# Expert input rows of a hybrid decoder step, picked by an indirect load instead of a selection product

## The reference, cut to what matters

```python
def _hier_moe(h, lp):                      # h: (tokens, 1024); 4 groups of 8 experts
    ...
    g_sel = jnp.argmax(g_logits, axis=-1)
    ...
    top_p, top_i = lax.top_k(jax.nn.softmax(e_logits, axis=-1), MOE_TOPK)      # 2 experts per token
    comb = p_group * top_p / jnp.sum(top_p, axis=-1, keepdims=True)
    expert = g_sel[:, None] * MOE_PER_GROUP + top_i
    w_tok = jnp.sum(jax.nn.one_hot(expert, MOE_EXPERTS) * comb[..., None], axis=1)
    gate = jnp.einsum('td,edf->tef', t, lp['w_exp_gate'])     # (32, 1024, 256)
    up = jnp.einsum('td,edf->tef', t, lp['w_exp_up'])         # (32, 1024, 256)
    act = jax.nn.silu(gate) * up * w_tok[..., None]
    out = jnp.einsum('tef,efd->td', act, lp['w_exp_down'])    # (32, 256, 1024)
```

## Time and profile before

| | |
|---|---|
| median of 3 runs | 901.95 us (899.47 to 902.05) |
| profiled execution | 901.02 us, of which the profile's span is 899.3 us |
| TensorE busy | 780.3 us (87%) |
| mean granted clock of TensorE | 0.935 of full |
| moved by DMA | 189.43 MB, of which 96 loads of 1024 KB are expert weights |

### The profile page before, as it was taken

How to read it: one execution, slowest core, us unless ns; L and a number is a source line. 1 busy time by engine, 2 the same in 40 slices (tenths; PEclk the granted TensorE clock), 3 DMA queues, 4 the chain that set the end, 5 groups by cost and what they waited for, 6 DMA issues and landing times.

```text
span 899.3 us, 21936 instructions
## 1 busy us (share of the span) xinstructions
PE 780.3 (87%) x9281; PEld 558.2 (62%) x9282; DVE 263.5 (29%) x731; ACT 222.0 (25%) x522; POOL 79.3 (9%) x187
## 2 busy tenths in 40 slices
PE   2679999999876689998988997569999999999984
PEld 2577777876664466776766775325556555655643
DVE  0044404411253465645611212431111111111123
ACT  1331131127413421521550003401111111111116
POOL 7000000010113210000000000011111111111100
PEclk9969999999977789999999999758999999999997
DMA  7826779994437754151026087407999975898201
GB/s 247 222 85 213 270 268 331 319 320 147 113 91 187 187 141 141 48 164 48 24 77 240 0 348 300 193 1 264 415 418 408 414 325 209 333 407 329 122 3 52
DMA packets 106471, 189.43 MB, mean 211 GB/s; under 512 B 9276, under 2 KB 70409, under 8 KB 98232
## 3 DMA queue, kind: packets, MB, share of 16 engines
q1 hardware_dynamic: 106424, 188.76, 59.0%
HBM read 180.16 MB, written 8.59 MB: 210 GB/s over the span
## 4 chain that ended last, share of the span: by engine, by line
PE 81%; DVE 7%; ACT 5%; DMA 3%; issue 3%; SPq 1%; POOL 0%; ACTq 0%; DVEq 0%; POOLq 0%
PE ps L1074 16%; PE ps L495 8%; PE ps L1232 7%; PE ps L443 6%; PE ps L461 5%; PE ps L510 4%; PE ps L408 3%; PE ps L1016 3%; PE ps L387 3%; PE ps L464 2%; PE ps L391 2%; PE ps L451 2%; DMA arena<-in_w_ada 1%; ACT arena L1460 1%; PE ps L503 1%
## 5 line engine op out<-in xcount | busy, mean ns | idle before, releaser
L1074 PE MATMUL ps<-arena 128*128 128x288 f32 x576 | 144.9, 412 | 0.0
L1074 PEld LDWEIGHTS ps<-arena 128*128 128x128 f32 x576 | 109.7, 193 | 31.0 <-DMA arena<-in_w_in 0.8
L495 PE MATMUL ps<-arena 128*32 128x128 f32 x2432 | 75.8, 278 | 12.5 <-issue 11.2
L495 PEld LDWEIGHTS ps<-arena 128*32 128x32 f32 x2432 | 66.2, 112 | 28.8 <-issue 27.7
L1232 PE MATMUL ps<-arena 128*128 128x288 f32 x256 | 71.1, 422 | 4.1 <-ACT arena L1583 4.1
L443 PE MATMUL ps<-arena 128*32 128x256 f32 (+1 forms) x936 | 64.4, 388 | 8.1 <-POOL arena L367 8.1
L1232 PEld LDWEIGHTS ps<-arena 128*128 128x128 f32 x256 | 47.1, 194 | 20.4 <-issue 8.8
L721 DVE TENSOR_SCALAR level<-arena 128x288 f32<-128x288 f32 x38 | 16.3, 429 | 114.4 <-PE ps L464 114.4
L443 PEld LDWEIGHTS ps<-arena 128*32 128x32 f32 (+1 forms) x936 | 26.3, 109 | 31.3 <-issue 25.1
L461 PE MATMUL ps<-level,arena 32*128 32x256 f32 x624 | 44.7, 401 | 0.5 <-DVE arena L724 0.5
L365 POOL TENSOR_TENSOR arena<-arena 128x192 f32<-128x192 f32 x39 | 20.5, 526 | 268.0 <-PE ps L443 234.2
(11 more groups left out here) (420 smaller groups left out, 1048.5 us busy)
## 6 DMA issues: line engine op xcount, KB each, us to landing
arena<-in_w_exp_gate SPq DMA_DIRECT2D x32, 1024.0 KB, 7.9
arena<-in_w_exp_up SPq DMA_DIRECT2D x32, 1024.0 KB, 10.0
arena<-in_w_exp_down SPq DMA_DIRECT2D x32, 1024.0 KB, 9.0
arena<-in_w_ada SPq DMA_DIRECT2D x12, 2048.0 KB, 10.2
arena<-in_w_in SPq DMA_DIRECT2D x18, 1024.0 KB, 6.0
arena<-in_w_ada_final SPq DMA_DIRECT2D x4, 2048.0 KB, 14.9
arena<-in_w_in SPq DMA_DIRECT2D x16, 512.0 KB, 4.0
arena<-in_state_ssm_rec SPq DMA_DIRECT2D x8, 512.0 KB, 6.8
```

Source lines behind the costliest of these rows:

```text
L495: l = mm(ps[CW * q:CW * (q + 1), 5, 0:P].rearrange("p (g f) -> p g f", g=2), xwin[:, at:at + CW], gate_up[:, :, k, f:f + HF], start=(k == ...
L1074: l = mm(ps[:, 2 + 2 * sl + m, 0:TOK], w_ring[sl][:, k, m * P:(m + 1) * P], HN[:, k, :], start=(k == 0), stop=(k == KT - 1))
```

## The change

The token rows `h2_tok` are stored to a memory tensor `h2_rows` of 1152 rows of 256 values (four rows for each token). VectorE makes row numbers `idx` from the place table. GpSimd fetches the 128 rows of a window by an indirect load into one of two buffers `xgs`, two windows ahead, and ScalarE copies them to `xg2`. The mask products and `picked_rows` are gone. `combined` stands behind the gate and up product. Windows are counted in pairs. The accumulators are cleared right behind the sums of the second norm, with `xT` as the other operand. The logits are transposed after the first 8 of the 24 token transposes, which now go through two banks. A seventh buffer `ex[6]` takes the place of `h2_tok` and of the routing's scratch, which moves elsewhere; its gate and up loads are issued once the rows are stored, its down load once the place tables are made. `sq3` takes the final squares.

```diff
-ESLOT = 6
+ESLOT = 7
...
         xg, q = carve(3 * DH * D, 2 * P)
+        xgs = (xg, carve(3 * DH * D + 8 * P + 2 * TOK, 2 * P)[0])
...
+        xg2, q = carve(q, 2 * P)
...
+        for at in (0, EXW, MIX, MIX + EXW, ex_at, ex_at + EXW, ex_at + 2 * EXW):
             wgu, at = carve(at, 2 * KT, FF)
-            wd, at = carve(at, FT, D)
+            wd, _ = carve(at if len(ex) < 6 else h2_at, FT, D)
...
+        assert at <= MIX
...
+        h2_rows = nc.dram_tensor("h2_rows", [4 * TOK, 2 * P], F32, kind="Internal").ap()
...
+            e.wait_ge(S("h2_tok"), 6)
+            for t, (o, p) in enumerate(TILES):
+                store(h2_rows[4 * o:4 * (o + p), :].rearrange("(p q) n -> p (q n)", q=4), h2_tok[0:p, t, :])
+            rec_stores.append(stores[0])
+            e.wait_ge(S("stored"), 16 * rec_stores[1])
+            wgu, wd = ex[6]
+            load(wgu[:, 0:KT, :], wg_[:, 6], "ex_ld6")
+            load(wgu[:, KT:2 * KT, :], wu_[:, 6], "ex_ld6")
+            e.wait_ge(S("count_mm"), 3)
             e.wait_ge(S("tab"), 1)
+            load(wd, wd_[:, 6], "ex_ld6")
             with e.Fori(1, E // ESLOT) as i:
...
+            for q in range(4):
+                link(g.memset(quarter[CW * q:CW * (q + 1)], float(q)))
...
-            def picked(n):
-
-                g.tensor_tensor(out=pm6, in0=B6, in1=A6[:, :, bass.ds(n, 1)].broadcast_to([P, 6, CW]), op=ALU.mult).then_inc(S("pm6"), 1)
-                e.wait_ge(S("pm6"), n + 1)
-                g.tensor_tensor(out=pm, in0=pm6[:, 0:3, :], in1=pm6[:, 3:6, :], op=ALU.add).then_inc(S("pm"), 1)
-
-            e.wait_ge(S("placed"), 1)
-            picked(0)
-            chunks = e.value_load(tab[0:1, 1, E - 1:E], min_val=1, max_val=MAXWIN)
-            with e.Fori(0, chunks) as c:
-                e.wait_ge(S("pick_mm"), c + 1)
-                e.wait_ge(S("pm"), c + 1)
-                picked(c + 1)
+            def gathered(rows, u):
+
+                g.indirect_dma_start(xgs[u], None, h2_rows, bass.IndirectOffsetOnAxis(rows, 0)).then_inc(S(f"xg_ld{u}"), 16)
+
+            e.wait_ge(S("stored"), 16 * rec_stores[1])
+            e.wait_ge(S("idx"), 1)
+            for u in range(2):
+                gathered(idx[:, u:u + 1], u)
+            e.wait_ge(S("tab"), 1)
+            pairs = e.value_load(tab[0:1, 2, 0:1], min_val=1, max_val=MAXWIN // 2)
+            with e.Fori(0, pairs) as c:
+                for u in range(2):
+                    e.wait_ge(S("xg"), c * 2 + (u + 1))
+                    g.tensor_copy(out=idx_now[:, u:u + 1], in_=idx[:, bass.ds(c * 2 + (u + 2), 1)]).then_inc(S("idx"), 1)
+                    e.wait_ge(S("idx"), c * 2 + (u + 2))
+                    g.tensor_tensor(out=idx_seen[:], in0=idx[0:1, 0:1], in1=idx[0:1, 0:1], op=ALU.add)
+                    gathered(idx_now[:, u:u + 1], u)
...
+            e.wait_ge(S("y_row"), 1)
+            for m in (1, 2, 3, 4, 0):
+                n = 4 * P if m < 4 else 2 * P
+                if m == 0:
+                    e.wait_ge(S("root"), 2)
+                l = mm(ps[:, m, 0:n], y_row[0:SMP, 0:P], xT[0:SMP, :, :].rearrange("p k n -> p (k n)")[:, 0:n], start=True, stop=False)
+            l.then_inc(S("comb_mm"), 1)
...
             for t, (o, p) in enumerate(TILES):
                 for half in range(2):
+                    if t:
+                        e.wait_ge(S("h2_tok"), 2 * t + half - 1)
                     for k in range(4):
-                        l = tr(ps[0:p, 2 + 2 * t + half if t < 2 else 6 + half, k * P:(k + 1) * P], H2[:, 4 * half + k, o:o + p], ident[:, :])
+                        l = tr(ps[0:p, 6 + half, k * P:(k + 1) * P], H2[:, 4 * half + k, o:o + p], ident[:, :])
                     l.then_inc(S("h2t_mm"), 1)
-            e.wait_ge(S("lg_row"), 1)
-            for t, (o, p) in enumerate(TILES):
-                l = tr(ps[0:p, 0, t * 36:(t + 1) * 36], lg_row[:, o:o + p], ident[0:EG + E, 0:EG + E])
-            l.then_inc(S("rt_mm"), 1)
+                if t == 0:
+                    e.wait_ge(S("lg_row"), 1)
+                    for u, (o_, p_) in enumerate(TILES):
+                        l = tr(ps[0:p_, 5, u * 36:(u + 1) * 36], lg_row[:, o_:o_ + p_], ident[0:EG + E, 0:EG + E])
+                    l.then_inc(S("rt_mm"), 1)
 
             e.wait_ge(S("routed"), 2)
...
-            def picked_rows(n):
-
-                e.wait_ge(S("pm"), n + 1)
-                for t, (o, p) in enumerate(TILES):
-                    for q in range(4):
-                        l = mm(ps[CW * q:CW * (q + 1), 6, 0:2 * P], pm[0:p, t, :], h2_tok[0:p, t, 2 * P * q:2 * P * (q + 1)],
-                               start=(t == 0), stop=(t == 2))
-                l.then_inc(S("pick_mm"), 1)
...
             e.wait_ge(S("h2_tok"), 6)
-            picked_rows(0)
-            e.wait_ge(S("placed"), 2)
-            for i in range(6):
-                p = TILES[i % 3][1]
-                for q in range(4):
-                    l = mm(ps[CW * q:CW * (q + 1), 7, 0:2 * NWIN], B6[0:p, i, :], AV[0:p, i].rearrange("p a w -> p (a w)"),
-                           start=(i == 0), stop=(i == 5))
-            l.then_inc(S("count_mm"), 1)
-            e.wait_ge(S("y_row"), 1)
-            for m in range(5):
-                n = 4 * P if m < 4 else 2 * P
-                l = mm(ps[:, m, 0:n], y_row[0:SMP, 0:P], h2_tok[0:SMP, 0, 0:n], start=True, stop=False)
-            l.then_inc(S("comb_mm"), 1)
+            for a in range(2):
+                e.wait_ge(S("placed"), a + 1)
+                for i in range(6):
+                    p = TILES[i % 3][1]
+                    for q in range(4):
+                        l = mm(ps[CW * q:CW * (q + 1), 6 + a, 0:NWIN], B6[0:p, i, :], AV[0:p, a, i, :], start=(i == 0), stop=(i == 5))
+                l.then_inc(S("count_mm"), 1)
             picked_transposed(0)
-            e.wait_ge(S("placed"), 3)
             e.wait_ge(S("comb_mm"), 1)
 
             def windows(first, end, s):
...
-                    picked_rows(c + 1)
+                    combined(c)
                     e.wait_ge(S("h_row"), c + 1)
-                    e.wait_ge(S("y_row"), c + 1)
                     for r in (slice(0, HF), slice(HF, P)):
                         l = mm(ps[r, 7, 2 * P:2 * P + HF], h_row[:], ident[:, r], start=True, stop=True)
                     l.then_inc(S("h_mm"), 1)
-                    combined(c)
                     picked_transposed(c + 1)
                     e.wait_ge(S("hact"), c + 1)
                     for a in range(FT):
...
+            e.wait_ge(S("tab"), 1)
...
-            def picked_copied(n):
-
-                e.wait_ge(S("pick_mm"), n + 1)
-                act(xg, ps[:, 6, 0:2 * P], ACT.Copy).then_inc(S("xg"), 1)
+            def rows_copied(i, u):
+
+                e.wait_ge(S(f"xg_ld{u}"), i * 16 + 16)
+                act(xg2, xgs[u], ACT.Copy).then_inc(S("xg"), 1)
 
...
-            picked_copied(0)
+            rows_copied(0, 0)
             window_copied(0)
+            rows_copied(0, 1)
             e.wait_ge(S("tab"), 1)
-            chunks = e.value_load(tab[0:1, 1, E - 1:E], min_val=1, max_val=MAXWIN)
-            with e.Fori(0, chunks) as c:
-                e.wait_ge(S("gu_mm"), c + 1)
-                act(h_row[:], ps[:, 5, 0:HF], ACT.Silu).then_inc(S("h_silu"), 1)
-                picked_copied(c + 1)
-                e.wait_ge(S("h_mm"), c + 1)
-                act(hact[:], ps[:, 7, 2 * P:2 * P + HF], ACT.Copy).then_inc(S("hact"), 1)
-                window_copied(c + 1)
+            pairs = e.value_load(tab[0:1, 2, 0:1], min_val=1, max_val=MAXWIN // 2)
+            with e.Fori(0, pairs) as i:
+                for u in range(2):
+                    e.wait_ge(S("gu_mm"), i * 2 + (u + 1))
+                    act(h_row[:], ps[:, 5, 0:HF], ACT.Silu).then_inc(S("h_silu"), 1)
+                    e.wait_ge(S("h_mm"), i * 2 + (u + 1))
+                    act(hact[:], ps[:, 7, 2 * P:2 * P + HF], ACT.Copy).then_inc(S("hact"), 1)
+                    window_copied(i * 2 + (u + 1))
+                    rows_copied(i + 1, u)
             for k in range(KT):
...
-            tt(A6, GE[:, :, 0:NWIN], GE[:, :, 1:NWIN + 1], ALU.subtract)
+            link(tt(A6, GE[:, :, 0:NWIN], GE[:, :, 1:NWIN + 1], ALU.subtract))
...
+            tt(AV[:, 0], A6, tid.rearrange("p c t -> p (c t)").unsqueeze(2).broadcast_to([P, 6, NWIN]), ALU.mult)
...
-            for a, val in enumerate((tid, r_m[:, 4:6, :])):
-                l = tt(AV[:, :, a, :], A6, val.rearrange("p c t -> p (c t)").unsqueeze(2).broadcast_to([P, 6, NWIN]), ALU.mult)
-            link(l)
-            e.nop().then_inc(S("placed"), 1)
+            tt(AV[:, 1], A6, r_m[:, 4:6, :].rearrange("p c t -> p (c t)").unsqueeze(2).broadcast_to([P, 6, NWIN]),
+               ALU.mult).then_inc(S("placed"), 1)
+            pairs = r_n[:, 0, 0:1]
+            link(stt(r_c[:, 0:MAXWIN // 2], iota[:, 0:MAXWIN // 2], 2.0, r_n[:, 3, E - 1:E].broadcast_to([P, MAXWIN // 2]),
+                     ALU.mult, ALU.is_le))
```

(12 more changed lines are left out.)

## The result

The changed kernel takes 850.89 us (median of 4 runs, 848.45 to 853.74), the kernel before 900.71 on the same chip: ratio 0.9446, 95% interval 0.9419 to 0.9474. The forecast was 841, with a range of 830 to 864. The profiled execution of after took 853.74; it is the longest of the four, and what follows is accounted by it: span 852.0 against 899.3, 47.3 us less.

A forecast was written before the change was run, and what follows sets the result against it. TensorE was taken to set the end before, by a small margin over the transfers. From 901.0 us, 9.5 less ahead of the loop and 50.6 less in it gave 840.9, predicted as 841, range 830 to 864.

The forecast's parts named there:

- the first product near 599: Start of the loop: the first window's gate and up product was to start at 599.3 us.
- the clearing ahead of 564: Ahead of the loop: the moved clearing was to run before ScalarE's modulation ends at 564.45, costing nothing there.
- the window of 5.4 us: In the loop: the gap of a window in TensorE's chain was to be 5.4 us.
- Ahead of the loop: Steps before the first window, such as clearing, line 443, transposes and first load, were to sum to -9.5 us.
- The first load and GpSimd's work: Ahead of the loop: the first indirect load was to add 4.5 us, with about 1 us for GpSimd's work.
- The term of 7.97 for the clearing: Ahead of the loop: moving the clearing was to take its 7.97 us off the chain.
- by TensorE alone the loop is 208.6: In the loop: 264.2 less 54.3 for line 443 and 1.3 for one pass boundary gives 208.6 us.
- The transfers' bound: In the loop: weights and rows at 411 GB/s were to set the end at 213.6 us, losing 5.0 of the gain.
- 1: Rival: the first load is late, or small loads cost more than their bytes; 845 to 858 us, chance 0.23.
- rival 2: In the loop: the two-window cycle of load, GpSimd and copy binds in part; 860 to 899 us, chance 0.11.
- Rival 3: In the loop: row loads wait on the DMA engines behind queued weights; slower, 920 us, chance 0.06.
- 4: Rival: row loads fit beside the weights for nothing, first load takes 3.3 us; 835 us, chance 0.16.

The follow-up runs named there:

- x_late: Changed kernel with the clearing of the accumulators put back behind the place table: 855.4 us, ratio 0.9467.
- x_wide_tiny: Changed kernel with gate and up as 16 products of 256 columns, half the terms left out, and loop refills cut to 512 B a partition: 836.69 us.
- x_shift2: Changed kernel where GpSimd waits for the window's combining products before copying the next row numbers, so the load starts at another time: 843.94 us, ratio 0.9378.
- x_wide: Changed kernel with gate and up as 16 products of 256 columns instead of 32 of 128, half the terms left out: 842.81 us, ratio 0.9343.
- x_one: Changed kernel with rows fetched one window ahead instead of two, their copy behind Silu: 889.45 us, ratio 0.9873.
- x_split: Changed kernel with each window's down product as 16 products of 128 columns instead of 8 of 256: 885.12 us, ratio 0.9839.
- x_unroll: Changed kernel with the loop over passes of seven experts written out, no branch between experts: 846.8 us, ratio 0.9363.

## Why the forecast was right, and where it was off

The range held the result, but by its width: 850.9 lies outside the 837 to 845 that were given to the forecast's own account. Of its signs, the first product near 599 (598.12), the clearing ahead of 564 (562.08) and the transfers' rate came; the window of 5.4 us did not (5.85), nor did 5 us of waiting for weights at the end.

**Ahead of the loop** -9.2, forecast -9.5. The terms: the clearing is covered as said, though not at full clock: the granted clock was 1.00 from 556 to 558, 0.72 from 558 to 560 and 0.50 from 560 to 562, and it took 5.65 us (I had 4 to 8). The first load and GpSimd's work took 0.82 + 3.07 = 3.9, forecast 4.5; the place table's first part 1.78 for 2.0. GpSimd's first indirect load took 1.18 us, the later ones 0.99, and the rows were there 3.1 us after it began. The 6 us that the Trainium skill (GPSIMD Engine Reference, Instruction dispatch) gives for a first call of freshly loaded code don't show in this trace; whether this load is such a call, no run here tells. The term of 7.97 for the clearing was right only together with the 4.5: x_late prices the move alone at 4.1.

**Loop** -38.2, forecast -50.6. The step that failed is "by TensorE alone the loop is 208.6", more exactly its window of 5.4. It took line 495's 1.95 us over unchanged. The removal of line 443 and the hand-overs are as said (x_wide_tiny: 210.9 for the loop by TensorE alone, 2.3 above the 208.6; `hact` costs nothing). What was missing is the break in line 520: it makes the product 0.33 to 0.51 us longer where the load starts up to 0.5 us into it, and 0.56 to 0.59 where the load starts 0.74 us into it. Added up over the trace, the products of line 520 behind the first take 14.4 us more than the 1.95 of a whole one. 210.9 + 14.4 = 225.3, and 226.0 was measured. I had weighed GpSimd's load only as a transfer and as a wait of ScalarE, and not as a neighbour of TensorE's product; no row of before had such a load.

**The transfers' bound**, 213.6: the forecast had it set the end of after, and it doesn't. It exists, but lies under TensorE's 226.0 with the breaks, so that the term decided nothing. Where the break is gone it sets the end: 216.4 in x_shift2, 217.4 in x_wide. The last weights are in at 804.13 - 594.01 = 210.1 (forecast 208.2), and 0.9 of issue stands behind. The 5.0 forecast as lost to it measure 6.1.

**Rivals.** 1: the row loads cost the DMA engines no more than their bytes (413 GB/s with them), and the first came early; its time, 845 to 858, holds the result for another reason, by luck. 2 and 3: in after ScalarE never waits for a landing in the loop, since two windows of lead (10.8 us) cover 6 to 8. x_one shows rival 2 with one window of lead: 39 us lost. Rival 3's landing behind the weights of 12.7 us doesn't come: 5.7 to 7.7 with the queue full. By the Trainium skill (DMA: Bandwidth & Descriptors, Queues, rings and completion order), each DMA engine serves its queues in turn; these landings agree. 4: fell on the break.

**Behind the loop** +1.6 where I said 0. 1.2 of it is in the sums of squares (7.01, 5.82 before), which depend on when the clock comes back. In after the granted clock was 0.50 from 830 to 834; in x_wide it stayed at 1.00 and they took 4.13. They took 5.55 in x_shift2, and 5.8 in six other runs with the change, so this is phase and no cost of the change.

## What to carry to other kernels

When a product is removed and a small transfer put in, look at what the new instruction stands beside, and not only at what waits for it: here a 1 us indirect load cost the neighbouring engine 0.3 to 0.6 us in a window, 14.4 in all, and one wait that moved it took 9.6 us off the profiled loop (1.1 of them by the clock), before the transfers became the bound. If an engine stops and its trace gives no cause, measure from the start of each neighbour's instruction to the moment at which it goes on: here one of these distances is the same, 1.3 us, in every window. Price the lead of a prefetch by its landing under full load (5.7 to 7.7 us here for 131 KB, 3.1 for the first, before whose start nothing was moving), and take the lead away in an experiment to see what it was worth. Two edits that hide each other, as the clearing and the first load do, can't be summed one by one.

## What the runs showed of the hardware

- The break itself: with GpSimd's indirect load (0.99 us) starting 0.1 to 0.7 us into a run of 32 products of 128 columns (64 rows), that run stops once, after 45 to 59 rows, and goes on at its old pace 1.29 to 1.34 us after the load's start; it takes 2.28 to 2.52 us instead of 1.95. With 16 products of 256 columns (x_wide) nothing is seen, nor in nearly all windows with the load 0.5 to 0.9 us ahead of the product (x_shift2).
- The product on two column groups instead of four takes 3.65 us instead of 1.93 for the same count and width.
- x_split's boundary of 7.5 us, where after has 1.5: eight more products in each of the eleven copies of the loop body, and 65 instruction packets instead of 36. x_unroll carries 55 and has no such wait. What makes the one expensive was not tried apart.
